# First block's output projection in three passes over high and low parts, with part of the splitting on GpSimd, and a layer's fourth weight unit split before the last add

## What is computed

```python
# first block
mix = jnp.concatenate([attn, ssm], axis=-1) @ w_out     # (512 x 1024) @ (1024 x 1024)
return x + gate[:, None, :] * mix
# second block, for l in range(2)
h = rmsnorm(x, norm_g[l]); proj = h @ w_in[l]           # 1024 x 4096
...
x = x + y @ w_out[l]
# and at the end: rmsnorm(x, final_g)
```

## Time and profile before

| what | us |
|---|---|
| median of 3 runs (lowest to highest) | 1050.81 (1049.45 to 1052.25) |
| the profiled execution | 1052.36 |
| its span | 1050.5 |
| TensorE busy in it | 986.9 (94%) |
| VectorE busy | 563.7 (54%) |
| ScalarE busy | 421.3 (40%) |
| GpSimd busy | 64.5 (6%) |
| mean granted TensorE clock | 0.978 |

### The profile page before, as it was taken

How to read it: one execution, slowest core, us unless ns; L and a number is a source line. 1 busy time by engine, 2 the same in 40 slices (tenths; PEclk the granted TensorE clock), 3 DMA queues, 4 the chain that set the end, 5 groups by cost and what they waited for, 6 DMA issues and landing times. The chain is left out here.

```text
span 1050.5 us, 13649 instructions
## 1 busy us (share of the span) xinstructions
PE 986.9 (94%) x5281; PEld 706.3 (67%) x5281; DVE 563.7 (54%) x1224; ACT 421.3 (40%) x928; POOL 64.5 (6%) x101
## 2 busy tenths in 40 slices
PE   3899999999899999899999999999899999998996
PEld 2346576745456544788678887788788678886785
DVE  3699498541687625334595344734333695244732
ACT  4121220132467512242493534833232492524821
POOL 2001310210000000000001000000000001000000
PEclk9899999999999999999899999999899899999998
DMA  9734246042460012234321423213043311533202
GB/s 363 266 120 84 76 64 227 5 157 80 160 161 2 2 64 76 76 109 132 84 73 41 133 90 103 97 57 117 25 128 111 98 58 41 140 101 109 74 1 80
DMA packets 81523, 104.63 MB, mean 100 GB/s; under 512 B 3746, under 2 KB 51922, under 8 KB 81443
## 3 DMA queue, kind: packets, MB, share of 16 engines
q1 hardware_dynamic: 75362, 81.24, 24.3%
q0 software_dynamic: 5808, 22.15, 7.7%
q10 hardware_dynamic: 288, 0.36, 0.1%
HBM read 98.37 MB, written 4.19 MB: 98 GB/s over the span
## 5 line engine op out<-in xcount | busy, mean ns | idle before, releaser
L1769 DVE TENSOR_TENSOR w_lo<-ring,w_hi 128x1024 fp32r<-128x1024 f32 x80 | 97.9, 1225 | 114.4 <-ACT w_hi L706 111.3
L838 PE MATMUL bank<-w_hi,hT_hi 128*128 128x512 f32 x320 | 127.4, 398 | 8.4 <-DVE w_lo L1769 7.0
L838 PE MATMUL bank<-w_hi,hT_lo 128*128 128x512 f32 x320 | 126.2, 394 | 0.0
L838 PE MATMUL bank<-w_lo,hT_hi 128*128 128x512 f32 x320 | 126.1, 394 | 0.0
L838 PE MATMUL bank<-hT_hi,w_hi 128*128 128x512 f32 x320 | 125.8, 393 | 0.0
L838 PE MATMUL bank<-hT_lo,w_hi 128*128 128x512 f32 x320 | 124.6, 389 | 0.0
L838 PE MATMUL bank<-hT_hi,w_lo 128*128 128x512 f32 x320 | 124.5, 389 | 0.0
L838 PE MATMUL bank<-ring,hT_t 128*128 128x512 f32 (+2 forms) x320 | 112.6, 512 | 0.6 <-PE bank L838 0.6
L838 PE MATMUL bank<-hT_t,ring 128*128 128x512 f32 x224 | 99.9, 603 | 2.1 <-DVE hT_t L1430 1.5
L838 PEld LDWEIGHTS bank<-ring,hT_t 128*128 128x128 f32 x320 | 60.4, 190 | 50.9 <-issue 46.4
L706 ACT ACTIVATE w_hi<-ring 128x1024 fp32r<-128x1024 f32 x80 | 84.6, 1058 | 11.6 <-PE bank L838 11.1
(11 more groups left out here) (275 smaller groups left out, 1464.1 us busy)
## 6 DMA issues: line engine op xcount, KB each, us to landing
ring<-in_w_in SPq DMA_DIRECT2D x64, 512.0 KB, 4.1
ring<-in_w_ada SPq DMA_DIRECT2D x4, 2048.0 KB, 9.7
ring<-in_w_in SPq DMA_DIRECT2D x4, 2048.0 KB, 10.6
bias_ring<-in_na_bias POOLq DMA_DIRECT2D x8, 1024.0 KB, 5.4
ring<-in_w_out SPq DMA_DIRECT2D x16, 512.0 KB, 3.6
arena<-in_w_ada SPq DMA_DIRECT2D x2, 2048.0 KB, 20.2
ring<-in_w_out SPq DMA_DIRECT2D x2, 2048.0 KB, 13.0
bias_ring<-in_t_bias POOLq DMA_DIRECT2D x8, 448.0 KB, 3.6
```

The source lines that it names most:

```text
L838: return pe.matmul(out, lhsT, rhs, start=first, stop=last)
L1769: dve.tensor_tensor(w_lo[:, u % 4], raw_w[:, u % 4], w_hi[:, u % 4].bitcast(fp32), SUB).then_inc(S["w_split"], 1)
```

## The change

- The projection of the first block becomes three-pass (`tile_wo`). The high part of `hT` goes to `a_hi`, its low part is written over `hT` itself (`hT_r` is the same memory); the high part of a weight unit goes to `o_hi` (four units), its low part over the weights in the ring (`ring_lo`).
- GpSimd splits strips 4 to 7 of `hT` and the four units of half 0, right after the last `ssm_ready`, during the attention. ScalarE and VectorE split strips 0 to 3 after the last `mix_out`, and the four units of half 1 at t = 3, as released by tile 3.
- Tiles 0 and 1 are made in the order: strips 4 to 7 of tile 0, of tile 1, strips 0 to 3 of tile 0, of tile 1. The turning of rows 0 and 1 moves from behind tile 6 to the middle of tile 7.
- In `norm_stats` and `residual` the split of unit 3 moves ahead of the square and of the add of tile 7.
- Five buffers of the second block change their places in memory.

```diff
+            pool.wait_ge(S["ssm_ready"], 4)
+            for f in range(4, KD):
+                pool.tensor_copy(a_hi[:, f, :], hT[:, f, :]).then_inc(S["ssm_hi"], 1)
+                pool.wait_ge(S["ssm_hi"], f - 3)
+                pool.tensor_tensor(hT_r[:, f, :], hT[:, f, :], a_hi[:, f, :].bitcast(fp32), SUB).then_inc(S["ssm_lo"], 1)
+            pool.wait_ge(arrive[CH_WO % SLOTS], landed(CH_WO))
+            for j in range(4):
+                pool.tensor_copy(wo_hi(j), wo_raw(0, j)).then_inc(S["wo_hi"], 1)
+                pool.wait_ge(S["wo_hi"], j + 1)
+                pool.tensor_tensor(wo_lo(0, j), wo_raw(0, j), wo_hi(j).bitcast(fp32), SUB).then_inc(S["wo_lo"], 1)
...
+            def split_wo(j):
+
+                act.wait_ge(S["wo_used" if j < 3 else "wo_done"], j + 1)
+                act.activation(wo_hi(j), wo_raw(1, j), ACT.Copy).then_inc(S["wo_hi"], 1)
+
             def norm_stats(r, place, u):
                 for t in range(8):
-                    if t == 3 and r:
+                    if t == 3:
                         for j in range(4):
-                            split_hi(u - 4 + j)
+                            split_hi(u - 4 + j) if r else split_wo(j)
                     if t == 7 and r < LAYERS:
                         split_hi(u)
                         split_hi(u + 1)
                         rows_hi(r, 0)
                         rows_hi(r, 1)
                         split_hi(u + 2)
+                        split_hi(u + 3)
                     square(8 * r + t + 1, t // 4, t % 4, t // 4 * 512, 512, place)
...
                 if r < LAYERS:
-                    split_hi(u + 3)
                     rows_hi(r, 2)
...
-            act.wait_ge(S["ssm_ready"], 4)
+            act.wait_ge(S["mix_out"], NT)
+            for f in range(4):
+                act.activation(a_hi[:, f, :], hT[:, f, :], ACT.Copy).then_inc(S["mix_hi"], 1)
+            act.wait_ge(arrive[(CH_WO + 1) % SLOTS], landed(CH_WO + 1))
             norm_stats(0, bank[3], 0)
...
-            pe.wait_ge(S["ssm_ready"], 4)
-            for t in range(8):
...
-                    ins = mm(bank[6 + t % 2][:, :], hT[:, k, i * P:(i + 1) * P], slot(CH_WO + c, KD, 512)[:, k, :], m == 0, m == KD - 1)
...
+            def tile_wo(t, steps):
+
+                c, i = divmod(t, 4)
+                tok = slice(i * P, (i + 1) * P)
+                for m in steps:
+                    k = OUT_ORDER[m]
+                    if t == 0:
+                        if m % 2 == 0:
+                            pe.wait_ge(S["wo_lo"], m // 2 + 1)
+                        pe.wait_ge(S["ssm_lo" if k >= 4 else "mix_lo"], k % 4 + 1)
+                    if t == 4 and m % 2 == 0:
+                        pe.wait_ge(S["wo_lo"], 4 + m // 2 + 1)
+                    if t == 7 and m == 4:
+                        rows_T(0, 0)
+                        rows_T(0, 1)
+                    ins = mm3(bank[6 + t % 2][:, :], (a_hi[:, k, tok], hT_r[:, k, tok]),
+                              (wo_hi(m // 2)[:, m % 2, :], wo_lo(c, m // 2)[:, m % 2, :]), k, m == 0, m == KD - 1)
+                    if t == 3 and m in (1, 3, 5):
+                        ins.then_inc(S["wo_used"], 1)
...
+            for t in range(2):
+                tile_wo(t, range(0, 4))
+            for t in range(2):
+                tile_wo(t, range(4, KD))
+            for t in range(2, 8):
+                pe.wait_ge(S["x_ready"], t - 1)
+                tile_wo(t, range(KD))
...
+            for f in range(4):
+                dve.wait_ge(S["mix_hi"], f + 1)
+                dve.tensor_tensor(hT_r[:, f, :], hT[:, f, :], a_hi[:, f, :].bitcast(fp32), SUB).then_inc(S["mix_lo"], 1)
...
+            def split_wo(j):
+
+                dve.wait_ge(S["wo_hi"], 4 + j + 1)
+                dve.tensor_tensor(wo_lo(1, j), wo_raw(1, j), wo_hi(j).bitcast(fp32), SUB).then_inc(S["wo_lo"], 1)
```

More of the change, by code:

```diff
@@ L83, in cut @@
             return view.rearrange("p (" + " ".join(dims) + ") -> p " + " ".join(dims), **dims)
+        with ExitStack() as low:
+            ring_lo = low.enter_context(nc.sbuf_tensor("ring_lo", [P, SLOTS * SLOT], fp32r))
         ring = sb("ring", SLOTS * SLOT)
@@ L107, in build @@
             csl_pad = cut(sb1("csl_pad", KD * 32)[:, :], k=KD, m=32)
+        with ExitStack() as mid:
+            sbm = lambda name, n: mid.enter_context(nc.sbuf_tensor(name, [P, n], fp32r))
+            hT_r = cut(sbm("hT_r", KD * T)[:, :], k=KD, t=T)
+            sbm("mid_gap", D + 5 * GP * (LC + 1) + 3 * GP * SC + 2 * NT * NH + 3 * HD)
+            o_hi = cut(sbm("o_hi", 4 * UNIT)[:, :], u=4, n=UNIT)
+            a_hi = cut(sbm("a_hi", KD * T)[:, :], k=KD, t=T)
         second = ctx.enter_context(ExitStack())
@@ L112, in build @@
         bias_ring = cut(sb2("bias_ring", 4 * 1024)[:, :], b=2, j=2048)
+        v2 = cut(sb2("v2", NT * 512)[:, :], i=NT, f=512)
+        y2 = cut(sb2("y2", NT * D)[:, :], i=NT, f=D)
         hT_hi, hT_lo = (cut(sb2(n, KD * T, fp32r)[:, :], k=KD, t=T) for n in ("hT_hi", "hT_lo"))
         w_hi, w_lo = (cut(sb2(n, 4 * UNIT, fp32r)[:, :], u=4, n=UNIT) for n in ("w_hi", "w_lo"))
-        v2 = cut(sb2("v2", NT * 512)[:, :], i=NT, f=512)
-        y2 = cut(sb2("y2", NT * D)[:, :], i=NT, f=D)
         prob2 = cut(ring[:, 0:SLOT], b=8, t=T)
@@ L247, in build @@
             "cs_exp", "cp_ready", "cp_T", "cp_evac", "gate_tanh",
-            "s1_done", "s1_taken", "e1_done", "p1_scaled", "t1_done", "t1_evac", "o1_done", "mix_out", "scores_done", "scores_taken",
+            "s1_done", "s1_taken", "e1_done", "p1_scaled", "t1_done", "t1_evac", "o1_done", "mix_out", "ssm_hi", "ssm_lo", "mix_hi", "mix_lo", "wo_hi", "wo_lo", "wo_used", "scores_done", "scores_taken",
             "exp_done", "mixed", "pT_done", "pT_evac", "o_done", "o_used", "mix_ready", "mixT_done", "mixT_evac",
@@ L329, in used_early, with wo_part, wo_raw, wo_lo @@
             return 3 * (len(BY_TOKENS) * l + sum(kind in BY_TOKENS for kind in KINDS[:g]))
+        def wo_part(v, c, j):
+            o = (CH_WO + c) % SLOTS * SLOT + OUT_ORDER[2 * j] * 512
+            return cut(v[:, o:o + UNIT], k=2, n=512)
+        def wo_raw(c, j):
+            return wo_part(ring, c, j)
+        def wo_lo(c, j):
+            return wo_part(ring_lo, c, j)
+        def wo_hi(j):
+            return cut(o_hi[:, j], k=2, n=512)
         LOADS = NAH // 2 + DAH
@@ L1222, in tile_tok @@
                 return ins
+            def tile_wo(t, steps):
[16 more added lines that the diff above has]
+                        ins.then_inc(S["wo_used"], 1)
+                if m == KD - 1:
+                    ins.then_inc(S["wo_done"], 1)
+            for t in range(2):
[5 more added lines that the diff above has]
+                tile_wo(t, range(KD))
+                if t % 4 == 3:
+                    pe.wait_ge(S["wo_done"], t + 1)
+                    pe.sem_inc(S["w_free"], 1)
             def na_score(l, m):
@@ L1797, in rows_lo @@
                                       hT_hi[:, at_[0], at_[1]].bitcast(fp32), SUB).then_inc(S["xT_lo"], 1)
+            def split_wo(j):
+                dve.wait_ge(S["wo_hi"], 4 + j + 1)
+                dve.tensor_tensor(wo_lo(1, j), wo_raw(1, j), wo_hi(j).bitcast(fp32), SUB).then_inc(S["wo_lo"], 1)
             def residual(r, add, u):
                 for t in range(8):
-                    if t == 3 and r:
+                    if t == 3:
                         for j in range(4):
-                            split_lo(u - 4 + j)
+                            split_lo(u - 4 + j) if r else split_wo(j)
                     if t == 7 and r < LAYERS:
@@ L1810, in residual @@
                         split_lo(u + 2)
+                        split_lo(u + 3)
                     add(t)
@@ L1815, in residual @@
                 if r < LAYERS:
-                    split_lo(u + 3)
                     rows_lo(r, 2)
```

## The result

| | us |
|---|---|
| before, median of 4 runs (lowest to highest) | 1051.02 (1049.45 to 1052.25) |
| after, median of 4 runs | 1033.49 (1031.98 to 1034.95) |
| ratio after to before, 95% interval | 0.983 (0.981 to 0.985) |
| profiled execution of after, its span | 1031.98, 1030.1 |

The change takes off 17.5 us, 1.7%; the forecast was 14.8 less and 1036.0.

What follows compares the result with a forecast made beforehand. TensorE, busy 94% of the span, was taken to bound the kernel. Gains 11.4 + 3.6 + 6.8 minus 7 for the attention gave 14.8 us less: 1036.0 us, range 1028 to 1046.

Steps and rivals of the forecast that it cites:

- part 5: GpSimd splits strips and weight units beside the attention, making VectorE multiplies wait: costs 7 us, bounds 2 and 14.
- Part 1: First block's output projection: 64 products go from 0.859 to 0.680 us each, 11.4 us off TensorE.
- Parts 2 and 3: Splitting the attention's half after its last write, and the second weight chunk during tile 3: both hidden, cost 0.
- Part 4: Layer starts: splitting the last unit before the add removes TensorE's stall and low clock; 3.6 us (layer 0), 6.8 (layer 1).
- the 1.1 us of new waits: Layer 0 start: short new waits of 0.4, 0.5 and 0.2 us along VectorE's chain, subtracted from the gain.
- rival (d): First projection: GpSimd's low parts come late, so the kernel is slower; at 6 ns a column 1062 us; chance 0.06.
- the upper total: GpSimd's splitting beside the attention: 26 us in all if a subtracted column takes 3 ns.
- the weighted half of an instruction: Attention: average wait of a pair's first VectorE multiply for the GpSimd instruction in progress, 0.75 us.
- (a): Attention: GpSimd rides free, its copies and subtractions not holding VectorE or falling into idle time; 1029 us; chance 0.20.
- (b): Attention suffers more: slow subtractions cost 14 us and TensorE's clock falls; 1043 us, or 1046 with the clock; chance 0.13.
- (c): Layer starts: the waits only change their name, row normalisations becoming the late ones; 4.4 us less, 1046; chance 0.06.
- (e): First block's output projection: the products don't become faster; 1047 us; chance 0.03.

Runs made afterwards that it cites:

- The exchange of the two buffers: The changed kernel with the buffers o_hi and a_hi exchanged in memory, nothing else; measured once at 1036.09 us.

## Why the prediction came out right, step by step

**The bound, and where a stall goes.** That TensorE's work and its two stalls are what can be won holds: every line of the ledger that became shorter by more than 0.7 us is one of those, save the first, which the change does not touch; the one that grew is the attention, as priced in part 5.

**Part 1 was mis-sized.** 11.4 was forecast and 10.2 measured: 8 tiles at 6.87 - 5.60 = 1.27 us. The step that failed is the tile of 5.44 us carried over from the second block. Weight loads of the same three-pass form, in this projection and in a second-block one, on after:

```profile
376.14 0.19 PEld L883 LDWEIGHTS bank<-o_hi,hT_r 128*128 128x128 f32 x1
376.37 0.19 PEld L883 LDWEIGHTS bank<-ring_lo,a_hi 128*128 128x128 f32 x1
...
377.77 0.19 PEld L883 LDWEIGHTS bank<-ring_lo,a_hi 128*128 128x128 f32 x1
```

```profile
689.92 0.19 PEld L883 LDWEIGHTS bank<-w_lo,hT_hi 128*128 128x128 f32 x1
690.15 0.19 PEld L883 LDWEIGHTS bank<-w_hi,hT_hi 128*128 128x128 f32 x1
...
691.73 0.19 PEld L883 LDWEIGHTS bank<-w_hi,hT_lo 128*128 128x128 f32 x1
```

1.63 us for 7 passes, 0.233 each, against 1.81 for 8, 0.226 each, both at a clock of 1.00. The exchange of the two buffers did not move it. Nor is it the DMA traffic: the median distance of two loads is 0.234 us over 364 to 376, where the DMA share is 0.06, and over 388 to 400, where it is 0.44. Why the passes of this stage are 3% slower stays open.

**Parts 2 and 3, as forecast.** The half strips of the attention and the second chunk's splits are hidden: TensorE's only wait in the projection is 0.30 us at 386.39, and the kernel before had 0.30 there too, when tile 4 took up the second chunk (389.44 in its trace).

**Part 4, right for layer 1 and short for layer 0.** Layer 1: 6.9 for 6.8; the whole of the low clock came back, as taken. Layer 0: 4.8 for 3.6. The stall and its clock gave 3.16 + 1.5 = 4.7 as priced; the step that failed is the 1.1 us of new waits of TensorE for the row normalisations. They did not come: the wait of 0.30 at 411.05 stood before layer 0 already (0.30 at 419.20 in the trace of before), and the earlier split alone shows 10.17 us against the whole change's 10.44. This error and that of part 1 cancel, 1.2 against 1.2, so the sum 15.0 of the two was right by chance.

**Part 5, right in kind and too dear.** 4.3 us measured, 7 taken, bounds 2 and 14. GpSimd's total was 22.2 us (309.21 to 331.43), not 17.5: the subtraction of 1024 columns took 2.37, not 1.86, the copy 1.18, not 0.98. That made it 7 steps and not 5.1. What was mis-sized is the price of one step: waits of 1.85 us a step were assumed. The 48 multiplies behind the last strip took 28.15 us in all, 19.70 before: 8.45, or 1.2 a step. The first multiply waits out the long subtraction, the second only the short copy, for the two alternate on GpSimd. Even the widest pairs, 2.50 for 0.87, waited 1.63 and not 1.85. Of these 1.2 half went into time in which VectorE had been idle, and 4.3 / 7 = 0.6 a step was left. Three inputs of this part and of rival (d) do not come out as given: the upper total is 25.3 us (26), the weighted half of an instruction 0.65 (0.75), and the 24 pairs take 19.7 us in before (17); none moves the 7 by more than 0.3. The Trainium skill, page "SBUF — State Buffer", section "Who interferes with whom", has the port held for a whole instruction; the trace agrees, for copies and subtractions alike: a multiply that met one ended 0.21 to 0.24 us after it. The trace also shows that the wait falls nearly all on VectorE, where a pair took up to 1.63 us more and a GpSimd copy 0.13. The Trainium skill, page "GPSIMD Engine Reference", section "Elementwise — side-by-side cycle accounting", gives 4497 ns for 2048 columns; 2.37 for 1024 agrees. The total of 20 us that the prediction estimated from it was nearer to the 22.2 than 17.5, but the cost of 8 further off than 7.

**The marks.** Of those that were named: multiplies of 1 us and more from 311, yes, until 332 and not 340; no TensorE wait over 1 us where a layer starts, and a clock of 1.00, yes; adds 5.44 apart, no, 5.60; first product at about 368, no, at 363.45 (2.7 us because the attention grew by 4.3 and not 7, and 2.2 because this run came earlier to it). Rivals (a) and (d) fell with pairs of multiplies of 2.50 us and with a first product that waited for nobody, (b) with the clock of 1.00 in the torn stretch, (c) with the earlier split alone, which kept its whole gain, and (e) with adds 5.60 us apart.

With 4.3 for 7 in the sum, 14.8 becomes 17.5, which is what the medians show. That it fits to a tenth is luck: the runs of either kernel spread over some 3 us.

## What to carry to other kernels

Before speeding up a stage, look for what the next engine's chain will show behind it: the three passes saved 10.2 us in their stage and gave 2.4 in all, since GpSimd's share of the splitting cost 4.3 in the attention and the start of the next layer grew by 2.35; with one split moved ahead of an add, that start grew no more and two stalls were gone. Work that is given to GpSimd beside VectorE multiplies like these should be let in once for each of VectorE's steps, behind the multiplies, and in pieces that end before the next ones; making the pieces small without that brought nothing here.

## What the runs showed of the hardware beyond that

GpSimd gave way very little beside a VectorE that was 99% busy: its subtractions of 1024 columns took 2.36 to 2.38 us, and a copy of 512 columns that began during a multiply 0.73 or 0.74 in place of 0.60 or 0.61. VectorE's multiplies stretched from 0.48 to 1.43 us and ended about 0.21 us after the GpSimd instruction that they had met. In the pair at 323.15 the two engines took turns: subtraction, multiply, copy, multiply. VectorE's score takes, which read a bank and the causal mask, kept 0.55 us beside the same instructions.

A TensorE that was busy 18.48 of 22.40 us in short pieces kept a clock of 1.00, while a single idle time of 5.00 us, up to 422.06 in the run of the three passes alone, came with the 1.2 GHz level (0.50) over 420 to 426, and one of 2.93 us without GpSimd's splitting with 0.54 over 364.3 to 368. And the same three-pass product ran 0.233 us a pass in one stage and 0.226 in another, which no run here explains.
